# Gated delta rule on raw keys and queries: lengths folded into beta, v and the output norm, and the carried state taken out between two token tiles

## The reference

```
qkv = silu(causal_depthwise_conv(x @ w_in))          # 8 key heads, 16 value heads of 128
q, k = l2norm(q), l2norm(k)                          # x * rsqrt(sum(x*x) + eps), eps = 1e-6
beta = sigmoid(b);  g = -exp(a_log) * softplus(a + dt_bias)
q = q * dk**-0.5
S_t = a_t S_(t-1) (I - b_t k_t k_t^T) + b_t k_t v_t^T ;   o_t = S_t^T q_t
o = o * rsqrt(mean(o*o) + eps) * norm_w * silu(z)
return o @ w_out
```

## Time and profile before

| what | us |
|---|---|
| three runs | 1450.56, 1451.86, 1452.66 |
| the profiled execution | 1453.67 |
| its span (first to last instruction) | 1451.7 |
| TensorE busy in the span | 1421.8 (98%) |
| VectorE, ScalarE, GpSimd busy | 1007.7, 839.6, 84.8 |
| mean granted clock of TensorE | 0.997 |

### The profile page before, as it was taken

How to read it: one execution, slowest core, us unless ns; L and a number is a source line. 1 busy time by engine, 2 the same in 40 slices (tenths; PEclk the granted TensorE clock), 3 DMA queues, 4 the chain that set the end, 5 groups by cost and what they waited for, 6 DMA issues and landing times.

```text
span 1451.7 us, 20276 instructions
## 1 busy us (share of the span) xinstructions
PE 1421.8 (98%) x8043; PEld 1165.1 (80%) x8043; DVE 1007.7 (69%) x1397; ACT 839.6 (58%) x1250; POOL 84.8 (6%) x170
## 2 busy tenths in 40 slices
PE   6999999999999999999999999999999999999998
PEld 5888878878888887788887888887778788788886
DVE  5887788766655766665557666567988876866555
ACT  6657574745444554554445554457878777554444
POOL 8000000000000000000000000000140410000000
PEclk9999999999999999999999999999999999999999
DMA  7532453336555555555555656545544332566562
GB/s 227 185 114 92 158 181 118 114 115 203 188 189 186 185 194 175 178 184 185 192 185 178 204 175 194 182 152 186 153 126 119 99 118 88 162 202 193 184 191 99
DMA packets 164189, 237.73 MB, mean 164 GB/s; under 512 B 17714, under 2 KB 110544, under 8 KB 164096
## 3 DMA queue, kind: packets, MB, share of 16 engines
q1 hardware_dynamic: 162400, 233.08, 49.6%
q0 software_dynamic: 1632, 3.35, 0.9%
q10 hardware_dynamic: 64, 0.02, 0.0%
HBM read 234.84 MB, written 1.57 MB: 163 GB/s over the span
## 4 chain that ended last, share of the span: by engine, by line
PE 90%; DVE 4%; ACT 3%; DMA 2%; issue 1%; SPq 0%; POOL 0%; ACTq 0%; DVEq 0%
PE A L245 17%; PE A L246 16%; PE A L247 16%; PE M L245 5%; PE G L245 5%; PE M L247 5%; PE G L247 5%; PE G L246 5%; PE M L246 5%; PE A L1267 1%; PE G L1188 1%; PE G L1235 1%; PE M L623 1%; DMA raw<-in_ffn_w_gate_up 1%; DVE gdn_gd_t L2700 1%
## 5 line engine op out<-in xcount | busy, mean ns | idle before, releaser
L227 DVE TENSOR_TENSOR w_lo<-raw,w_hi 128x1024 fp32r<-128x1024 f32 (+2 forms) x296 | 506.6, 1732 | 172.7 <-ACT w_hi L209 172.0
L209 ACT ACTIVATE w_hi<-raw 128x1024 fp32r<-128x1024 f32 (+2 forms) x296 | 428.0, 1461 | 168.9 <-DMA raw<-in_ffn_w_gate_up 137.2
L245 PE MATMUL A<-w_hi,x_hi 128*128 128x512 f32 (+1 forms) x640 | 261.1, 408 | 5.6 <-DVE x_lo L419 2.9
L247 PE MATMUL A<-w_hi,x_lo 128*128 128x512 f32 (+1 forms) x640 | 248.5, 388 | 0.0
L246 PE MATMUL A<-w_lo,x_hi 128*128 128x512 f32 (+1 forms) x640 | 247.6, 387 | 0.0
L245 PEld LDWEIGHTS A<-w_hi,x_hi 128*128 128x128 f32 x640 | 121.0, 189 | 36.7 <-DVE x_lo L419 8.2
L247 PEld LDWEIGHTS A<-w_hi,x_lo 128*128 128x128 f32 x640 | 120.8, 189 | 25.5
L662 ACT ACTIVATE ffn_ffn_e<-ffn_ffn_z 128x512 f32<-128x512 f32 x44 | 27.8, 632 | 195.4 <-DVE ffn_ffn_z L696 195.4
L245 PE MATMUL A<-w_hi,ffn_ffn_hT_hi 128*128 128x512 f32 x352 | 138.7, 394 | 0.0
L246 PEld LDWEIGHTS A<-w_lo,x_hi 128*128 128x128 f32 x640 | 121.4, 190 | 21.4 <-issue 1.0
L246 PE MATMUL A<-w_lo,ffn_ffn_hT_hi 128*128 128x512 f32 x352 | 138.4, 393 | 0.0
(11 more groups left out here) (385 smaller groups left out, 2077.3 us busy)
## 6 DMA issues: line engine op xcount, KB each, us to landing
raw<-in_ffn_w_gate_up SPq DMA_DIRECT2D x176, 512.0 KB, 4.7
raw<-in_ffn_w_down SPq DMA_DIRECT2D x88, 512.0 KB, 4.2
raw<-in_w_in SPq DMA_DIRECT2D x48, 512.0 KB, 4.3
raw<-in_gdn_w_in SPq DMA_DIRECT2D x48, 512.0 KB, 4.5
raw<-in_sc_w_in SPq DMA_DIRECT2D x24, 512.0 KB, 4.7
raw<-in_w_out SPq DMA_DIRECT2D x16, 512.0 KB, 4.7
raw<-in_gdn_w_out SPq DMA_DIRECT2D x16, 512.0 KB, 4.3
raw<-in_w_mem_kv SPq DMA_DIRECT2D x8, 512.0 KB, 5.1
```

The source lines that it names most:

```text
L209: ins = act.activation(net.w_hi[:, v % RING, part], net.raw[:, v % RING, part], ACT.Copy)
L227: ins = dve.tensor_tensor(net.w_lo[:, v % RING, part], net.raw[:, v % RING, part], net.w_hi[:, v % RING, part].bitcast(F32), ALU.subtract)
L245: pe.matmul(out, xh, hi[:, k, c, :], start=start and k == 0, stop=False)
L247: mm = pe.matmul(out, xl, hi[:, k, c, :], start=False, stop=stop and k == nk - 1)
```

## The change

- The multiply of silu writes q and k, unnormalised, straight into qT and kT; the squares are taken from there. kk and qk therefore wait for silu and no longer for the norm.
- A norm sums with the squares as the weights and one column of ones as the moving side, so the sums stand by token in 4 numbers a partition, not in 512. For k, ScalarE makes 1/length^2 (inv_k) and length (root_k), and VectorE multiplies beta by inv_k. For q the sum is only copied and turned into the eps of the output norm (q_eps).
- vt scales v by root_k, in two copies. kd waits for the scaled beta. z2 takes its Ln per group with q_eps as the bias.
- In the core no state is formed: p0 multiplies k0 with k1 and with q1 (the tiles' keys and queries), in place of the transpose of k; p1 loses its two state products and the copy; p2 applies these two matrices to the scaled v of tile 0. p3 takes over the wait for the copy of tile 0's output.
- conv and silu wait for less before they use t and sg again, since the norm does not read them any more.
- GDN_ORDER, the sequence of steps, is not touched.

```diff
@@ -2022,6 +2022,7 @@
...
         self.norms = [x for x in self.steps if x[0] == "norm"]
+        self.k_norms = [x for x in self.norms if x[1][0] == "k"]
@@ -2033,6 +2034,11 @@
...
         return 1 if step[0] == "ba" else int(step[2])
+    def raw_of(self, c, part):
+        first = 4 * int(c[1]) + 2 * part
+        return (self.qT if c[0] == "q" else self.kT)[:, first:first + 2, :]
@@ -2053,8 +2059,9 @@
...
         self.ss16 = net.sb("gd_ss", [P, TT * 4])
+        self.root_k, self.inv_k = (net.sb(f"gd_{n}", [P, TT, GH]) for n in ("root_k", "inv_k"))
+        self.q_eps = net.sb("gd_q_eps", [P, TT, GH])
         self.qT, self.kT = net.sb("gd_qT", [P, GH, T]), net.sb("gd_kT", [P, GH, T])
-        self.kn = net.sb("gd_kn", [P, 2, P])
@@ -2293,14 +2300,16 @@
...
     pe.wait_ge(*self.squared(self.l2s.index((c, step[2])) + 1))
-    pe.matmul(bank[:, :], self.ones[:, :],
-              self.sg[:, 2 * part:2 * part + 2, :].rearrange("p k t -> p (k t)"),
-              start=True, stop=True).then_inc(self.bank_pe[self.half_of(step)].sem, 1)
+    for t in range(TT):
+        for k in range(2):
+            mm = pe.matmul(bank[:, 2 * t + k:2 * t + k + 1], self.sg[:, 2 * part + k, t * P:(t + 1) * P],
+                           self.ones[:, 0:1], start=True, stop=True)
+    mm.then_inc(self.bank_pe[self.half_of(step)].sem, 1)
...
     bank = self.take(pe, step)
-    pe.wait_ge(*self.l2(self.norms.index(("norm", f"k{g // 4}", str(g % 4 // 2))) + 1))
+    pe.wait_ge(*self.silued(self.silus.index((f"k{g // 4}", str(g % 4 // 2))) + 1))
@@ -2314,7 +2323,8 @@
...
     pair = int(step[1])
-    pe.wait_ge(*self.l2(self.norms.index(("norm", f"q{pair // 2}", str(pair % 2))) + 1))
+    for c in (f"k{pair // 2}", f"q{pair // 2}"):
+        pe.wait_ge(*self.silued(self.silus.index((c, str(pair % 2))) + 1))
@@ -2428,7 +2438,8 @@
...
 pe.wait_ge(*self.bank_act[g % 2](self.reads(step)))
-pe.transpose(bg[:, tile(2)], kT[:, tile(0)], net.ident[:, :])
+pe.matmul(bg[:, tile(2)], kT[:, tile(0)], kT[:, tile(1)], start=True, stop=True)
+pe.matmul(bg[:, tile(3)], kT[:, tile(0)], qT[:, tile(1)], start=True, stop=True)
@@ -2437,15 +2448,13 @@
...
 for j in range(2):
-    pe.matmul(bm[:, tile(j)], self.QK[g][:, 2 * j, :], self.vn[i][:, j, :], start=True, stop=True)
-    mm = pe.matmul(bm[:, tile(2 + j)], self.kn[:, i, :], self.S[g][:, 2 + j, :],
-                   start=True, stop=True)
+    mm = pe.matmul(bm[:, tile(j)], self.QK[g][:, 2 * j, :], self.vn[i][:, j, :], start=True, stop=True)
         elif x == "p2":
+carried = self.S[g][:, 2:4, :].rearrange("p j e -> p (j e)")
+pe.matmul(bg[:, 0:T], self.S[g][:, 0, :], carried, start=True, stop=True)
+mm = pe.matmul(bg[:, T:2 * T], self.S[g][:, 1, :], carried, start=True, stop=True)
+        elif x == "p3":
 pe.wait_ge(*act(8))
-S = self.S[g][:, 0:2, :].rearrange("p j e -> p (j e)")
-pe.matmul(bg[:, 0:T], kT[:, tile(1)], S, start=True, stop=True)
-mm = pe.matmul(bg[:, T:2 * T], qT[:, tile(1)], S, start=True, stop=True)
-        elif x == "p3":
@@ -2529,7 +2538,7 @@
...
         else:
-            act.wait_ge(*self.l2(self.norms.index(("norm",) + before) + 1))
+            act.wait_ge(*self.silued(n - 1))
@@ -2545,13 +2554,20 @@
...
     act.wait_ge(*self.silued(self.silus.index(step[1:3]) + 1))
-    act.activation(self.sg[:, half, :], self.t[:, half, :], ACT.Square).then_inc(self.squared.sem, 1)
+    act.activation(self.sg[:, half, :], self.raw_of(step[1], int(step[2])), ACT.Square).then_inc(self.squared.sem, 1)
 elif kind == "norm":
+    c, first = step[1], 4 * int(step[1][1]) + 2 * int(step[2])
     bank = self.written(act, step)
-    half = self.sg[:, 2 * int(step[2]):2 * int(step[2]) + 2, :].rearrange("p k t -> p (k t)")
-    act.activation(half, bank[:, :], ACT.Ln, bias=EPS).then_inc(self.bank_act[self.half_of(step)].sem, 1)
+    sums = bank[:, 0:2 * TT].rearrange("p (t k) -> p t k", t=TT)
+    if c[0] == "q":
+        act.activation(self.q_eps[:, :, first:first + 2], sums, ACT.Copy)\
+           .then_inc(self.bank_act[self.half_of(step)].sem, 1)
+        continue
+    root, inv = (m[:, :, first:first + 2] for m in (self.root_k, self.inv_k))
+    act.activation(root, sums, ACT.Ln, bias=EPS).then_inc(self.bank_act[self.half_of(step)].sem, 1)
     act.wait_ge(*self.bank_act[self.half_of(step)](self.reads(step)))
-    act.activation(half, half, ACT.Exp, scale=-0.5).then_inc(self.rsq.sem, 1)
+    w.chain(act.activation(inv, root, ACT.Exp, scale=-1.0))
+    act.activation(root, root, ACT.Exp, scale=0.5).then_inc(self.rsq.sem, 1)
@@ -2562,8 +2578,14 @@
...
     first = 512 * int(step[1][1]) + T * int(step[2])
-    act.activation(self.v[:, :, first:first + T], bank[:, :].rearrange("p (t n) -> p t n", t=TT), ACT.Copy)\
-       .then_inc(self.bank_act[self.half_of(step)].sem, 1)
+    g = 2 * int(step[1][1]) + int(step[2])
+    act.wait_ge(*self.rsq(self.k_norms.index(("norm", f"k{g // 4}", str(g % 4 // 2))) + 1))
+    for t in range(TT):
+        ins = act.activation(self.v[:, t, first:first + T], bank[:, t * T:(t + 1) * T], ACT.Copy,
+                             scale=self.root_k[:, t, g:g + 1])
+        if t == 0:
+            w.chain.mark(ins)
+    ins.then_inc(self.bank_act[self.half_of(step)].sem, 1)
@@ -2579,8 +2601,14 @@
...
     act.wait_ge(*self.o_sq(2 * i + tt + 1))
+    act.wait_ge(*self.l2(self.norms.index(("norm", f"q{i // 2}", str(i % 2))) + 1))
     ss = self.ss16[:, 4 * tt:4 * tt + 4]
-    w.chain(act.activation(ss, ss, ACT.Ln, scale=1.0 / P, bias=EPS))
+    for one in range(2):
+        own = self.ss16[:, 4 * tt + 2 * one:4 * tt + 2 * one + 2]
+        g = 2 * i + one
+        ins = act.activation(own, own, ACT.Ln, scale=1.0 / P, bias=self.q_eps[:, tt, g:g + 1])
+        w.chain.mark(ins)
+    w.chain.sync()
@@ -2627,15 +2655,14 @@
...
 act.wait_ge(*pe(8))
-w.chain.mark(act.activation(self.kn[:, i, :], bg[:, tile(2)], ACT.Copy))
+w.chain.mark(act.activation(self.S[g][:, 0:2, :], bg[:, T:2 * T], ACT.Copy))
...
 act.wait_ge(*pe(9))
-w.chain.mark(act.activation(self.v[:, 0, heads], bm[:, 0:T], ACT.Copy))
-ins = act.activation(self.S[g][:, 0:2, :], bm[:, T:2 * T], ACT.Copy)
+ins = act.activation(self.v[:, 0, heads], bm[:, 0:T], ACT.Copy)
@@ -2713,23 +2740,31 @@
...
         if n >= 2 and self.silus[n - 2][0][0] != "v":
-            dve.wait_ge(*self.l2(self.norms.index(("norm",) + self.silus[n - 2]) + 1))
+            dve.wait_ge(*self.bank_act[int(step[2])](self.reads(("norm",) + self.silus[n - 2])))
...
         dve.wait_ge(*self.sigm(n + 1))
-        dve.tensor_tensor(self.t[:, half, :], self.t[:, half, :], self.sg[:, half, :], ALU.mult)\
+        dst = self.t[:, half, :] if step[1][0] == "v" else self.raw_of(step[1], int(step[2]))
+        dve.tensor_tensor(dst, self.t[:, half, :], self.sg[:, half, :], ALU.mult)\
...
     c, part = step[1], int(step[2])
-    dve.wait_ge(*self.rsq(self.norms.index(step) + 1))
-    half = slice(2 * part, 2 * part + 2)
+    dve.wait_ge(*self.bank_act[self.half_of(step)](self.reads(step)))
     first = 4 * int(c[1]) + 2 * part
-    dst = (self.qT if c[0] == "q" else self.kT)[:, first:first + 2, :].rearrange("p k t -> p (k t)")
-    dve.scalar_tensor_tensor(out=dst, in0=self.t[:, half, :].rearrange("p k t -> p (k t)"),
-                             scalar=P ** -0.5 if c[0] == "q" else 1.0,
-                             in1=self.sg[:, half, :].rearrange("p k t -> p (k t)"),
-                             op0=ALU.mult, op1=ALU.mult).then_inc(self.l2.sem, 1)
+    if c[0] == "q":
+        sums = self.q_eps[:, :, first:first + 2]
+        dve.tensor_scalar(sums, sums, P * EPS, P * EPS * EPS + EPS, ALU.mult, ALU.add).then_inc(self.l2.sem, 1)
+        continue
+    dve.wait_ge(*self.rsq(self.k_norms.index(step) + 1))
+    dve.wait_ge(*self.ba["act"](1))
+    for k in range(2):
+        h = 2 * (first + k)
+        ins = dve.tensor_tensor(self.beta[:, :, h:h + 2], self.beta[:, :, h:h + 2],
+                                self.inv_k[:, :, first + k:first + k + 1].to_broadcast([P, TT, 2]), ALU.mult)
+        if k == 0:
+            w.chain.mark(ins)
+    ins.then_inc(self.l2.sem, 1)
@@ -2744,6 +2779,7 @@
...
     dve.wait_ge(*self.k_exp(self.kks.index(step[1:3]) + 1))
+    dve.wait_ge(*self.l2(self.norms.index(("norm", f"k{g // 4}", str(g % 4 // 2))) + 1))
```

## The result

The changed kernel takes 1457.5 us (median of 17 runs, 1453.85 to 1466.08), the kernel before in the same series 1452.2 (17 runs): ratio 1.0038, 95% interval 1.0024 to 1.0051. It is slower, by 5.3 us, where the forecast had it 1.9 us faster. Its profiled execution took 1458.82 us (span 1456.6, mean granted clock 0.993, against 0.997).

A forecast was written before the change was run, and what follows sets the result against it. TensorE, busy 98% of the span, bounds the kernel; the 1039 to 1055 chain (-1.1), core groups (-0.2, -0.4, -0.45) and small losses (+0.1 three times) sum to -1.9 us: median 1450.0, range 1446.5 to 1454.0.

The forecast's parts named there:

- The norm's price: TensorE's norm matmuls: eight one-column passes take 0.90 us against 0.87 before, 0.3 us dearer over eight norms.
- Rival (c): Norms on TensorE: narrow passes are cheap (0.010 us each), 6.6 us less, 1443.4; chance 0.04.
- Core steps: TensorE's p0 +0.34 us, p1 -0.45 a group, p2 unchanged; net -0.9 us over eight groups.
- ScalarE and VectorE: Gated-delta stage: ScalarE 5.3 us lighter, VectorE about 4.5; worth nothing where TensorE is the chain.
- The 1039.5 to 1055 chain: Waits through ScalarE and VectorE around the q0 norms get shorter: gain 1.1 us.
- Is it kept?: At GpSimd's masked copy of U, 16 us later: the 1.1 us gain just fits, 0.1 given back.
- Rival (a): GpSimd's chain to 1071.66 does not move, the 1.1 us become waiting: -0.8, 1451.0; chance 0.17 with (e).
- (b): Four TensorE waits after 1055, together 2.8 us, vanish as ScalarE and VectorE are lighter: 1447.2; chance 0.15.
- (d): Added small ScalarE work at vt, p0 and z2, 1100 to 1230, is exposed: +3.8 us, 1455.7; chance 0.11.
- (e): The change does not do what it says; only the -0.6 us of passes, 1451.3; chance 0.17 with (a).
- The two waits for VectorE's corrections: TensorE's waits for VectorE's corrections of U and T, 1.7 us together, stay.
- cores 2 and 3's -0.4: vt steps +0.5, p0's extra passes free inside TensorE's 0.5 us wait at core 2's p1, p1 steps -0.9: -0.4 us.

The follow-up runs named there:

- the early padding: Changed kernel with 40 unused tiny matmuls in TensorE's first wait of the gated-delta stage: 1452.1 us, ratio 0.9992.
- the filler besides: Changed kernel with the 40 early tiny matmuls and eight unused wide matmuls ahead of the wait at core:0:k1: 1453.6 us, ratio 1.0004.
- the version with the later k1 of core 0: Changed kernel with the 40 early tiny matmuls and core:0:k1 one quarter of a weight slot later: 1451.1 us, ratio 0.9994.

## Why the prediction was wrong

- **The norm's price: right.** The timeline of the changed kernel, against the earlier trace rows:
```profile
1006.41 0.39 PE L247 MATMUL A<-w_hi,x_lo 128*128 128x512 f32 x1
1006.63 0.95 PE L2305 MATMUL A<-gdn_gd_ones,gdn_gd_sg 128*128 128x1 f32 x8
...
1007.76 0.39 PE L246 MATMUL A<-w_lo,x_hi 128*128 128x512 f32 x1
```
1.35 - 0.46 = 0.89 us (forecast 0.90). Rival (c) is out. The 25 ns that the prediction took from the Trainium skill's "TensorE: Matmul & The Clock Gate", section "Back-to-back issue gap", are the gap of an isolated matmul, and the same section says that this formula has no budget for the weight load; with a weight load for each one-column pass the trace has 0.112 us a pass.
- **Core steps: right.** Eight passes of two p1 steps take 0.89 us where sixteen took 1.79. The run with the new core alone (1451.6 against 1452.2) agrees with the forecast 0.9 but does not part it from nothing.
- **ScalarE and VectorE: sizes off, without effect.** ScalarE fell by 3.4 us, not 5.3 (vt's copies take 0.476 each, the two small Ln of z2 0.287 each, not 0.20), VectorE by 6.0, not 4.5.
- **The 1039.5 to 1055 chain: right.** TensorE reached k1 1.5 us sooner (forecast 1.1), and neither wait around the q norms is left.
- **"Is it kept?": the step that failed.** It said that the spread is released by TensorE's weight load and that the gain just fits by 0.06 us; "if GpSimd's solve ended later the gain would be gone here". It ended 2.7 us later, and where the sum had 0.1 us given back, k1 ran 2.3 us later than before, behind a wait of 4.4 us. The solve was taken as fixed in time. Its start hung on a DMA, and the fetch of TensorE's instructions, which the change had moved, delayed it by 1.3 us. Its length depends on which of its passes meet VectorE's: it was 16.9 us for 15.4, and 14.9 in the changed kernel once it started on time. A GpSimd pass of 128x28 took 0.25 us before and 1.11 where it met the first low-part subtraction of VectorE. The Trainium skill ("SBUF — State Buffer", section "SBUF: two separate sides") says that such a two-input operation and GpSimd exclude each other for a whole instruction; the trace agrees (the pass of 1.11 us ends 0.1 us after the subtraction that began before it).
- **Rival (a) had the mechanism and the wrong price.** It priced the case of a gain given back at 0.8 us less than before. The sum had no term for the granted clock: all rows read before had 1.00, and that was taken as a constant. The wait of 4.4 us had a second price of about its own size (up to 5 us behind it). The Trainium skill ("TensorE: Matmul & The Clock Gate", section "Why this matters for your kernels") warns of idle gaps between bursts of matmuls; the trace agrees for the gap of 4.4 us, and shows the fall behind gaps of 1.8 to 2.7 us as well.
- **The stop in t2 was in no rival.** The count of added matmuls (40 more records over the kernel) was read as time only, not as a shift of the instruction stream.
- **Rivals (b), (d), (e)** are out. No wait for vt or z2 appeared. The two waits for VectorE's corrections shrank to 0.9 only where the stop lay ahead of them; with the early padding they are 1.7 again, as forecast. There p1 waits 0.8 us for VectorE, where the forecast had its 0.5 filled by p0's passes: that part of cores 2 and 3's -0.4 was not got. The 64 one-column records and p1's halved passes stand in the trace, so the change does what it says.

## What to carry to other kernels

Where a side engine's round trip ends within a microsecond of the main engine, ask what can delay the side engine, not only what releases it; the gain won ahead of it may turn into a wait, and a wait of some microseconds on TensorE can cost nearly twice its length (4.2 us more of wait, 7.5 of time). Adding or removing some fifty TensorE instructions moves every fetch of its instructions: look at the place of "issue" gaps inside dense runs of tiny matmuls, and try a little padding in an existing wait before judging a change of a few microseconds.

## What the runs showed of the hardware

TensorE's instructions come in pieces of 16 KB, most of them taking about 1 us (0.9 to 2.0 in the traces). In a run of 32x32 matmuls the border between two pieces stopped the engine for 1.8 to 2.7 us, and one such piece delayed another transfer's eight packets by 1.1 us. The clock also fell in changed kernels behind short waits at k1 or none: 1.0 us with the early padding, none with the filler besides, 0.4 in the version with the later k1 of core 0, whose stretch 1072 to 1080 follows. One-column norms and tiny tiles lie in it; whether they are the reason was not tested.
```profile
1072.00:1080.00 8.00, 8.00 (x168) 6.88 (x168) 5.74 (x16) 1.97 (x7) 3.47 (x2) 0.57 0.31 117
```
